# Feed-forward stage in four token quarters instead of two halves, with weight remainders on GpSimd

## What is computed

```python
def conv_ffn(x, w_up, conv_w, conv_b, w_down):
    s_len = x.shape[1]
    u = x @ w_up
    up = jnp.pad(u, ((0, 0), (CONV_W - 1, 0), (0, 0)))
    c = conv_b + sum(up[:, j:j + s_len] * conv_w[j] for j in range(CONV_W))
    gte, val = c[..., :D_FF], c[..., D_FF:]
    return (jax.nn.gelu(gte) * val) @ w_down
...
ffn = conv_ffn(x, w_up[l], conv_w[l], conv_b[l], w_down[l])
x = layer_norm(ALPHA * x + ffn, ln2_g[l], ln2_b[l])
```

## Time and profile before

| | us |
|---|---|
| median of 3 runs | 5037.99 (5034.23 to 5044.51) |
| span of the profiled execution | 5034.6 |
| feed-forward stage in it | 1957.2 |
| TensorE busy over the span | 3830.0 (76%) |
| VectorE busy | 2735.9 (54%) |
| ScalarE busy | 1465.2 (29%) |
| POOL busy | 163.3 (3%) |

### The profile page before, as it was taken

How to read it: one execution, slowest core, us unless ns; L and a number is a source line. 1 busy time by engine, 2 the same in 40 slices (tenths; PEclk the granted TensorE clock), 3 DMA queues, 4 the chain that set the end, 5 groups by cost and what they waited for, 6 DMA issues and landing times. The chain is left out here.

```text
span 5034.6 us, 41358 instructions
## 1 busy us (share of the span) xinstructions
PE 3830.0 (76%) x14920; PEld 2867.8 (57%) x14920; DVE 2735.9 (54%) x4193; ACT 1465.2 (29%) x1843; POOL 163.3 (3%) x153
## 2 busy tenths in 40 slices
PE   2498999960278788836758886999999759999995
PEld 2344777750145455514436665777777647777774
DVE  1045788787466665536655553544444454544545
ACT  1144634455233344423332221211211111121120
POOL 0000100100000000000000000000000000000000
PEclk9756999985578899956669997999999879999997
DMA  6211222210210100021124443111111021111110
GB/s 129 63 42 62 69 82 90 87 54 20 60 36 21 28 21 7 5 65 36 34 81 142 135 137 89 51 38 49 39 47 42 30 98 41 38 51 38 38 51 38
DMA packets 292641, 287.24 MB, mean 57 GB/s; under 512 B 34917, under 2 KB 248549, under 8 KB 287270
## 3 DMA queue, kind: packets, MB, share of 16 engines
q1 hardware_dynamic: 257934, 233.93, 16.2%
q10 hardware_dynamic: 31968, 42.47, 2.5%
q0 software_dynamic: 2560, 8.39, 0.6%
HBM read 209.25 MB, written 75.50 MB: 57 GB/s over the span
## 5 line engine op out<-in xcount | busy, mean ns | idle before, releaser
L88 PE MATMUL ffn_up<-ffn_xh,ffn_uh 128*128 128x512 f32 x1536 | 597.7, 389 | 3.5 <-DVE ffn_xl L1316 3.5
L89 PE MATMUL ffn_up<-ffn_xl,ffn_uh 128*128 128x512 f32 x1536 | 597.5, 389 | 0.0
L90 PE MATMUL ffn_up<-ffn_xh,ffn_ul 128*128 128x512 f32 x1536 | 597.5, 389 | 0.0
L88 PE MATMUL ffn_dn<-ffn_dh,ffn_hh 128*128 128x512 f32 x768 | 325.4, 424 | 156.2 <-DVE ffn_acc L1301 135.0
L1305 DVE TENSOR_TENSOR ffn_ul<-ffn_ur,ffn_uh 128x1024 fp32r<-128x1024 f32 x96 | 117.6, 1225 | 584.2 <-ACT ffn_uh L1256 584.2
L1301 DVE TENSOR_TENSOR ffn_acc<-ffn_dn,ffn_acc 128x1024 f32<-128x1024 f32 x192 | 232.8, 1222 | 288.0 <-PE ffn_dn L90 288.0
L428 ACT ACTIVATE sel_junk<-sel_scs,sel_cand 128x768 bf16<-128x768 f32 (+5 forms) x186 | 270.0, 1452 | 349.2 <-DVE sel_cand L509 348.2
L88 PE MATMUL sel_acc<-xhi,sel_whi 128*128 128x512 f32 x864 | 341.1, 395 | 37.7 <-POOL sel_wlo L450 37.7
L89 PE MATMUL sel_acc<-xlo,sel_whi 128*128 128x512 f32 x864 | 340.1, 394 | 0.0
L90 PE MATMUL sel_acc<-xhi,sel_wlo 128*128 128x512 f32 x864 | 339.5, 393 | 0.0
L88 PEld LDWEIGHTS ffn_up<-ffn_xh,ffn_uh 128*128 128x128 f32 x1536 | 288.3, 188 | 63.5 <-DVE ffn_xl L1316 3.9
(11 more groups left out here) (207 smaller groups left out, 7071.2 us busy)
## 6 DMA issues: line engine op xcount, KB each, us to landing
ffn_ur<-in_w_up_dram SPq DMA_DIRECT2D x96, 512.0 KB, 6.1
zt<-sel_out ACTq DMA_DIRECT2D x27, 1024.0 KB, 3.9
ffn_dr<-in_w_down_dram SPq DMA_DIRECT2D x48, 512.0 KB, 3.6
att_raw<-zt SPq DMA_DIRECT2D x64, 256.0 KB, 4.1
mrg_gr<-zt SPq DMA_DIRECT2D x64, 256.0 KB, 4.3
sel_wraw<-in_w_in_dram ACTq DMA_DIRECT2D x27, 512.0 KB
prj_xin<-in_x_dram SPq DMA_DIRECT2D x16, 512.0 KB, 5.3
yt<-att_y POOLq DMA_DIRECT2D x32, 256.0 KB, 2.8
```

What stands on the lines that cost most here:

```text
L88: pe.matmul(out, ahi, bhi, start=first, stop=False)
L89: pe.matmul(out, ahi, blo, start=False, stop=False)
L90: return pe.matmul(out, alo, bhi, start=False, stop=last)
```

## The change

The stage now takes the tokens in four quarters of 512 (`TQ`), each of 4 blocks. There are 96 steps instead of 48, each with two up products over 512 tokens (one bank each, `up[:, a, k % 2]`, so four tiles are in flight). Other differences:

- Down products come in groups of `G = 4` feature tiles, four parts (token blocks) of 24 matmuls each. The table `after` says behind which step each group stands: within a quarter after steps 5, 9, 13, 17, 23 and 25, the last of them in the next quarter. In the last quarter the last two groups both stand behind the last step.
- Up weights have three buffers, and are loaded, copied and subtracted three tiles ahead of their product. Down weights have four for each of `dr`, `dh`, `dl`. Tables `early` and `late` say in which step the down tiles of the next group are split: two in the step behind a group, two at the head of the next.
- All weight remainders (`ul`, `dl`) are made on POOL, no longer on VectorE.
- `acc` is double: the next quarter's tokens are loaded in step 12 of the quarter before, and its transposes go into the banks of `up`, between the parts of the quarter's fifth down group. The multiplication by `ALPHA` is part of the first add of a block.
- Normalization of a quarter stands in steps 2 to 6 of the next. `hl` of a step is made in the next step of VectorE.
- SP issues tokens and three up tiles ahead of the tables of the convolution and the norm.

The diff, cut to its core (`...` marks what is left out). `up_high` and `down_high` are ScalarE's, `up_low` and `down_low` POOL's, `conv` to `normalize` VectorE's, `up_tile`, `down` and the rest TensorE's:

```diff
-        NH, TH = 2, SEQ // 2
-        TB = TH // P
-        G, R = 2, 3
+        NQ, TQ, TB, G, R = 4, CH, 4, 4, 8
+        NG = FT // G
+        STEPS = NQ * FT
...
+        after = {}
+        for q in range(NQ):
+            for g, t in enumerate((5, 9, 13, 17, 23, 25)):
+                after.setdefault(min(q * FT + t, STEPS - 1), []).append(q * NG + g)
+        lead = {J + 1: k for k, Js in after.items() for J in Js}
+        early, late = {-1: [0, 1], 0: [2, 3]}, {}
+        for J in range(1, NQ * NG):
+            if lead[J] + 1 < STEPS:
+                early[lead[J] + 1] = [G * J, G * J + 1]
+                late[lead[J] + 2] = [G * J + 2, G * J + 3]
+            else:
+                late.setdefault(STEPS, []).extend(range(G * J, G * J + G))
...
+            def up_high(w):
+                act.wait_ge(S[f"ul{w % 3}"], 16 * (w // 3 + 1))
+                if w >= 3:
+                    act.wait_ge(S["um"], w - 2)
+                    act.wait_ge(S["uld"], w - 2)
+                act.activation(uh[:, w % 3], ur[:, w % 3], ACT.Copy).then_inc(S["uhd"], 1)
+
+            def down_high(d):
+                act.wait_ge(S[f"dld{d % G}"], 16 * (d // G + 1))
+                if d >= G:
+                    act.wait_ge(S["dm"], TB * (d // G))
+                act.activation(dh[:, d % G, :], dr[:, d % G, :], ACT.Copy).then_inc(S["dhd"], 1)
...
+                for d in late.get(k, []):
+                    down_high(d)
+                for a in range(2):
+                    evacuate(k, a)
+                    if 2 * k + 3 + a < 2 * STEPS:
+                        up_high(2 * k + 3 + a)
+                    for d in early.get(k, [])[a:a + 1]:
+                        down_high(d)
...
+            def up_low(w):
+                pool.wait_ge(S["uhd"], w + 1)
+                pool.tensor_tensor(ul[:, w % 3], ur[:, w % 3], f32(uh[:, w % 3]), ALU.subtract).then_inc(S["uld"], 1)
+
+            def down_low(d):
+                pool.wait_ge(S["dhd"], d + 1)
+                pool.tensor_tensor(dl[:, d % G, :], dr[:, d % G, :], f32(dh[:, d % G, :]), ALU.subtract).then_inc(S["dsd"], 1)
...
+                conv(k, 0)
+                if k:
+                    hidden_low(k - 1)
+                conv(k, 1)
+                gate(k)
...
+                for J in after.get(k, []):
+                    for b in range(TB):
+                        add_down(J, b)
+                if q and 2 <= t < 2 + TB:
+                    moments((q - 1) * TB + t - 2)
+                if q and 3 <= t < 3 + TB:
+                    normalize((q - 1) * TB + t - 3)
...
+            def up_tile(k, a):
+                w = 2 * k + a
+                pe.wait_ge(S["uld"], w + 1)
+                if k % FT == 0:
+                    pe.wait_ge(S["xld"], (k // FT + 1) * 2 * TB)
+                elif k >= 2:
+                    pe.wait_ge(S["ue"], w - 3)
...
+            def down(J, b):
+                v = J * TB + b
+                if b == 0:
+                    pe.wait_ge(S["hs"], G * (J + 1))
+                    pe.wait_ge(S["dsd"], G * (J + 1))
+                if v >= 2:
+                    pe.wait_ge(S["da"], v - 1)
...
+                if t == FT - 1 and q + 1 < NQ:
+                    J = after[k][0]
+                    for g, b in ((0, -1), (1, 0), (2, -1), (3, -1), (4, -1), (5, 1), (6, -1), (7, 2)):
+                        transposes(q + 1, g)
+                        if b >= 0:
+                            down(J, b)
+                    down(J, 3)
```

More of the change, by code:

```diff
@@ L1252, in _ @@
+            for b in range(TB):
+                store((NQ - 1) * TB + b)
+            sp.wait_ge(S["st"], 16 * TB * NQ)
         @block.scalar
         def _(act):
[L1254 to L1284, removed]
@@ L1294, in link, with token_low @@
                 dve.wait_ge(S["dvl"], links)
[L1296 to L1305, removed]
+            def token_low(q, g):
+                b, half = g // 2, g % 2
+                a, par = bank[g % 4]
+                dst = slice(4 * half, 4 * half + 4), slice(b * P, (b + 1) * P)
+                dve.wait_ge(S["xhd"], q * 2 * TB + g + 1)
+                dve.tensor_tensor(xl[:, dst[0], dst[1]], up[:, a, par, :].rearrange("p (j f) -> p j f", j=4),
+                                  f32(xh[:, dst[0], dst[1]]), ALU.subtract).then_inc(S["xld"], 1)
@@ new lines, in moments @@
+            def moments(v):
+                q, b = v // TB, v % TB
+                row = acc[:, q % 2, b, :]
+                dve.wait_ge(S["da"], (q * NG + NG - 1) * TB + b + 1)
+                for i in range(2):
+                    last = dve.bn_stats(stat[:, i, :], row[:, i * CH:(i + 1) * CH])
+                link(last)
+                link(dve.bn_aggr(mv[:, v % 2, :], stat[:]))
+                dve.tensor_scalar(mv[:, v % 2, 1:2], mv[:, v % 2, 1:2], EPS, None, ALU.add).then_inc(S["ms"], 1)
@@ L1307, in _, with normalize @@
+            def normalize(v):
+                row = acc[:, (v // TB) % 2, v % TB, :]
+                dve.wait_ge(S["pw"], v + 1)
+                link(dve.tensor_scalar(row, row, mv[:, v % 2, 0:1], rstd[:, v % 2:v % 2 + 1], ALU.subtract, ALU.mult))
+                link(dve.tensor_tensor(row, row, gb[:, 0, :], ALU.mult))
+                dve.tensor_tensor(row, row, gb[:, 1, :], ALU.add).then_inc(S["od"], 1)
             dve.memset(mhalf[:], -0.5).then_inc(S["mhd"], 1)
-            up_weights(0, 0)
@@ new lines, in transposes @@
+            def transposes(q, g):
+                b, half = g // 2, g % 2
+                a, par = bank[g % 4]
+                if g == 0:
+                    pe.wait_ge(S["ax"], 16 * (q + 1))
+                if g >= 4:
+                    pe.wait_ge(S["xld"], q * 2 * TB + g - 3)
+                elif q:
+                    pe.wait_ge(S["ue"], 2 * (q * FT - 2 + par) + a + 1)
+                for j in range(4):
+                    kk = 4 * half + j
+                    last = pe.transpose(up[:, a, par, j * P:(j + 1) * P], acc[:, q % 2, b, kk * P:(kk + 1) * P], ident[:])
+                last.then_inc(S["tr"], 1)
```

351 lines of the change are left out of this document (198 added, 153 removed).

## The result

The change takes 4917.26 us (median of 4 runs, 4910.39 to 4923.3) against 5041.25 us (4 runs, 5034.23 to 5047.03) on the same chip: a ratio of 0.9756, with a 95% interval of 0.9741 to 0.9771. It is 2.4% faster. I had forecast 5000 us, 0.75% faster. The direction and the range held; the size did not.

The account below looks back on a forecast made before the run. TensorE's matmuls, 1568 us of the stage's 1957.2, were taken to set the pace. Start, matmuls, transposes, last weights and end gave 4723 us; with L = 278 that made 5001, said as 5000, range 4820 to 5085 (8 in 10).

Parts of the forecast that it names:

- L: What TensorE loses at the 24 down groups, waits and clock together; forecast 278 us, 217 before the change.
- waits at the groups: TensorE's waits at the down groups over the whole stage, without the clock's share; forecast 233 us.
- clock: Extra time from TensorE's granted clock falling after waits at the groups; forecast one us per group in most, 45 us.
- C1: Up tile whose weights POOL has at 31.4 us, TensorE wanting them at 27.2; forecast 4.2 us lost per group.
- D1: Later up tile whose weights come at 43.7 us where TensorE wants them at 42.05; forecast 1.6 us lost.
- first add: VectorE's add of a down group's first part, done by 63.4 us; TensorE wants that bank at 60.0, 3.4 us lost.
- Sum 9.2: Total of the three forecast TensorE waits in one followed group, 4.2, 1.6 and 3.4 us; 110 us for 12 plain groups.
- turns at the ports: VectorE and POOL each wait for the other at SBUF; if only VectorE waited, a group would lose about 7 us.
- T: Zero of the walk through one group: the moment the previous down group ends.
- step A: First up step after the previous down group, tiles A0 and A1; VectorE was forecast to end it at 21.5 us.
- rival A: Ports hardly matter, POOL gets in only at real gaps of VectorE; L = 96, 4820 us; chance 0.24.
- old wait: TensorE's 6.25 us wait at a down group before the change, begun before VectorE has come to its adds.

Follow-up runs that it names:

- the first experiment: The change with all weight remainders, up and down, moved from POOL back to VectorE; 4731.34 us, ratio to the kernel before 0.9392.

## Why the prediction was right and where it failed

**Right.** The form of the sum, time = 4723 + L, held: with L = 11, and 5.9 us in place of 10.7 for the last group's weights, the first experiment should take 4730 and took 4731. Its terms one by one:

| term | forecast | measured |
|---|---|---|
| first issue to first up product | 23.6 | 21.25 |
| transposes at the quarters | 12 | 12 |
| wait for the last group's weights | 10.7 | 10.6 |
| behind the last matmul | 28 | 27.5 |
| waits at the groups | 233 | 141 |
| clock | 45 | 52 (193 less 141) |
| L | 278 | 193 |

(141 is the sum of the gaps between matmuls beyond their pace; the rows of waits above, without the 10.6, give 132, as each is some 0.15 us short of its gap.) The places of the waits were right too: C1's remainder, D1's, and the first add. That the measured 4917 lies inside the stated range owes much to the width of that range, 265 us.

**Wrong: the step that failed is the walk through one group, "Sum 9.2", and the values set beside it for the other groups.** A plain group loses about 5 us: 2.2 to 2.4 at C1 (4.2 forecast), 0 to 0.8 at D1 (1.6), 1.7 to 2.8 at the add (3.4). A group that follows two steps behind another loses 5.3 at its own weights (7 to 8), one with normalizations about 16 (22). Only the first group went the other way, 8.0 us where 3.5 was forecast. The mechanism, turns at the ports, is the one shown above; as I read it the size was off because the walk added delays up. It also counted the gate among the operations that POOL blocks, and none of its 96 rows met POOL. It had C1 ready at T + 31.4, the gate of step A done at T + 21.5, the first add done at T + 63.4; they were T + 29.5, 20.6 and 60.3. A wait is the small difference of two large times: 1.9 us too much in 31 makes 4.2 out of 2.2, and 24 groups multiply it. I carried a pessimist's value at each turn into a sum to which each wait adds directly, and so got 278. The 193 measured lies about midway between that and rival A's 96, and rival A's reason is not what made it smaller: VectorE's short operations do not keep POOL out.

**Wrong in its account of the old wait.** "The group comes two tiles after its last input. That takes the old 6.25 us wait away": the groups one step earlier show that in a plain group it goes without that distance, if VectorE makes the remainders; beside POOL's this was not run.

**Missed.** I asked what POOL's remainders would cost TensorE, but not what VectorE would do with them. It was busy for 48% of a half and had room for all 288 at 1.22 us. The move costs 186 us, more than the whole gain of the change as measured.

**The rule of the Trainium skill.** I had weighed turns against a VectorE that alone waits, 9 us a group against 7; the measured 5 lies under both, so the time does not tell them apart. The rows do. Those above (POOL's 2.66, 2.86, 2.84 against 2.39 alone) show POOL waiting, which the prediction had named as a sign: on this the trace agrees with the Trainium skill (SBUF — State Buffer, section "SBUF: two separate sides"), that whichever of the two starts first holds the shared ports for its whole instruction. That page of the Trainium skill names operations of VectorE in a two-port fast mode or with two SBUF inputs. The blocked tensor_scalar has one, but 512 columns more cost it only 0.27 us (807 ns against 542), where scalar_tensor_tensor needs 0.53 (1284 against 752). So it goes through its columns twice as fast, which fits such a mode; no run here shows the mode itself. I had counted it as blocked by its row alone.

**Not settled.** The walk was not redone with the measured turns, so how much of the 2 us at C1 is POOL's earlier start and how much shorter VectorE stretches is argued, not shown.

## What to carry to other kernels

Before moving elementwise work from VectorE to GpSimd, ask whether VectorE is truly short of time: in these runs a GpSimd operation that reads SBUF cost its own time *and* stalled the VectorE operations that read only SBUF where they met, and was stalled by them. Price such a move as added work on both engines, and test it by moving the work back, one kind at a time. When a forecast multiplies a wait by the number of times it occurs, give it the middle of its bounds and show what half a microsecond does to the sum.

## What the runs showed of the hardware that I had not expected

- Work that nobody waits for, on the engine with the most room (558 rows of POOL, 940 us busy), slowed the whole kernel by 439 us. Part of it is TensorE's clock: its granted clock over the middle of the stage is 0.92 there and 1.00 in the first experiment.
- Operations of VectorE with a single SBUF tensor input are blocked by POOL as well: 2.16 us for a copy of two elements that takes 0.17 alone, 2.70 us for a tensor_scalar of 512 columns that takes 0.54. Operations with one input in PSUM and one in SBUF are not. The adds can't show it, as none of them starts while POOL runs, but the token remainders can, `ffn_xl<-ffn_up,ffn_xh`: in the change 9 of the 32 start while POOL runs and take 678 to 692 ns, as they do alone (680 to 692). Two of them in 1.29 us, in the middle of two rows of POOL:

```profile
3496.97 4.75 POOL L1330 TENSOR_TENSOR ffn_ul<-ffn_ur,ffn_uh 128x1024 fp32r<-128x1024 f32 x2 [5.84 <-ACT ffn_uh L1267]
3498.84 1.29 DVE L1376 TENSOR_TENSOR ffn_xl<-ffn_up,ffn_xh 128x512 fp32r<-128x512 f32 x2 [4.05 <-ACT ffn_xh L1279]
```

- TensorE's clock after short waits went either way for waits of the same length. Windows of PE (us, busy, granted clock, DMA share) behind waits of 2.19, 2.32, 2.19 and 2.21 us:

```profile
3239.50:3243.00 3.50, 3.44 (x15) 1.00 0.67 204
3270.40:3273.90 3.50, 3.50 (x15) 1.00 0.00 0
...
3311.00:3314.50 3.50, 3.50 (x9) 0.52 0.72 219
...
3382.40:3385.90 3.50, 3.49 (x9) 0.53 0.65 204
```

The first and the third stand at the same place of two groups, behind equal waits: one is at 2.4 GHz, the other at 1.2. Between the first and the last matmul of the stage it fell 25 times, mostly for 3.4 us, 119 us in all; in the two halves of the kernel before it fell 24 times, 191 us in all. The 12 slow matmuls of the earlier trace rows, 5.3 us, are from one of those. What decides it stays open; no run here tests it.
